# Second block: q's root mean square as a per-row scale of the attention's mask operation, norm weights applied at the eviction, rotary partners of q and k fetched by DMA

## The reference, cut to what matters

```python
def rmsnorm(x, g):
    xf = x.astype(jnp.float32)
    xf = xf * lax.rsqrt(jnp.mean(xf * xf, axis=-1, keepdims=True) + EPS)
    return (xf * g.astype(jnp.float32)).astype(x.dtype)

def rope(t, cos, sin):
    tf = t.astype(jnp.float32)
    t1, t2 = jnp.split(tf, 2, axis=-1)
    out = jnp.concatenate([t1 * cos - t2 * sin, t2 * cos + t1 * sin], axis=-1)
    return out.astype(t.dtype)

def diff_attention(q, k, v, lam):
    ...
        s = jnp.einsum('bqhcd,bkhcd->bhcqk', qblk, k).astype(jnp.float32) * scale
        s = jnp.where(mask, s, neg)
        p = jax.nn.softmax(s, axis=-1)
        a = p[:, :, 0] - lam * p[:, :, 1]
...
        xn = rmsnorm(h, norm1_gain[i])
        proj = xn @ w_in[i]
        q, k, v, u, gates = jnp.split(proj, splits, axis=-1)
```

## Time and profile before

| | |
|---|---|
| median of 3 runs (lowest, highest) | 2210.58 us (2198.4, 2211.85) |
| the profiled execution: its time, its span | 2207.66 us, 2205.9 us |
| TensorE busy, mean granted clock | 97% of the span, 0.986 |
| DVE, ACT, POOL busy | 49%, 40%, 42% |
| DMA | 194.99 MB, mean 88 GB/s |
| q and k phase, p = 0 to 31 | 1305.4 to 1463.8 us from the span's start |
| v, gated unit, projection, p = 32 to 59 | 1463.8 to 1572 us |
| attention and output | from 1572.5 us |

### The profile page before, as it was taken

One profiled execution on the slowest core, in us unless ns is written; L12 is line 12 of the kernel. 1 busy time (PEld: TensorE's weight loads), 2 busy tenths in 40 slices (PEclk: granted clock), 3 DMA queues, 4 the chain that ended last, 5 costly groups with the idle time before them and its releaser, 6 DMA issues.

```text
span 2205.9 us, 28059 instructions
## 1 busy us (share of the span) xinstructions
PE 2146.6 (97%) x10228; PEld 1689.7 (77%) x10228; DVE 1070.1 (49%) x1726; ACT 893.1 (40%) x1248; POOL 923.1 (42%) x306
## 2 busy tenths in 40 slices
PE   7999999999999998999999999999999899999999
PEld 6875788888888775888888887666666687888887
DVE  7854242222247635332222267857677723644645
ACT  5345462223243445543222343255466525332332
POOL 4523344444455322545654556323221245344442
PEclk9999999999999999999999999999999999999999
DMA  4422122322224311232232231111211222323232
GB/s 166 156 77 76 52 80 83 108 94 95 84 85 151 111 55 56 62 111 95 83 108 95 81 142 58 58 58 62 69 47 58 93 98 69 105 95 95 95 95 76
DMA packets 114679, 194.99 MB, mean 88 GB/s; under 512 B 4752, under 2 KB 50064, under 8 KB 114320
## 3 DMA queue, kind: packets, MB, share of 16 engines
q1 hardware_dynamic: 112992, 189.12, 26.0%
q10 hardware_dynamic: 1584, 4.53, 0.6%
HBM read 189.44 MB, written 8.12 MB: 90 GB/s over the span
## 4 chain that ended last, share of the span: by engine, by line
PE 75%; issue 17%; DVE 3%; POOL 3%; ACT 1%; DMA 0%; ACTq 0%; DVEq 0%; POOLq 0%; SPq 0%
PE bank L709 62%; PE bank L811 4%; POOL w_lo L516 3%; PE bank L820 2%; PE bank L1020 1%; PE bank L787 1%; PE bank L883 1%; PE bank L763 1%; PE bank L843 1%; PE bank L871 1%; PE bank L772 1%; PE bank L1034 0%; DVE act_lo L2041 0%; PE bank L913 0%; PE bank L1041 0%
## 5 line engine op out<-in xcount | busy, mean ns | idle before, releaser
L516 POOL TENSOR_TENSOR w_lo<-raw,w_hi 128x2048 fp32r<-128x2048 f32 (+1 forms) x167 | 742.0, 4443 | 1178.0 <-ACT w_hi L1361 1177.8
L709 PE MATMUL bank<-act_hi,w_hi 128*128 128x512 f32 x1488 | 600.8, 404 | 10.6 <-DVE act_lo L2041 5.4
L709 PE MATMUL bank<-act_lo,w_hi 128*128 128x512 f32 x1488 | 583.6, 392 | 0.0
L709 PE MATMUL bank<-act_hi,w_lo 128*128 128x512 f32 x1488 | 583.5, 392 | 0.0
L1361 ACT ACTIVATE w_hi<-raw 128x2048 fp32r<-128x2048 f32 (+1 forms) x170 | 314.0, 1847 | 560.0 <-PE bank L709 541.2
L709 PEld LDWEIGHTS bank<-act_hi,w_hi 128*128 128x128 f32 x1488 | 282.3, 190 | 86.5 <-issue 14.6
L709 PEld LDWEIGHTS bank<-act_lo,w_hi 128*128 128x128 f32 x1488 | 282.2, 190 | 61.6 <-issue 5.3
L709 PEld LDWEIGHTS bank<-act_hi,w_lo 128*128 128x128 f32 x1488 | 281.7, 189 | 60.7
L709 PE MATMUL bank<-h_hi,w_hi 128*128 128x512 f32 x704 | 279.4, 397 | 0.3 <-DVE x L2462 0.3
L709 PE MATMUL bank<-h_hi,w_lo 128*128 128x512 f32 x704 | 277.9, 395 | 0.0
L709 PE MATMUL bank<-h_lo,w_hi 128*128 128x512 f32 x704 | 277.9, 395 | 0.0
(11 more groups left out here) (361 smaller groups left out, 2733.2 us busy)
## 6 DMA issues: line engine op xcount, KB each, us to landing
raw<-in_w_up SPq DMA_DIRECT2D x32, 1024.0 KB, 5.4
raw<-in_w_down SPq DMA_DIRECT2D x32, 1024.0 KB, 5.0
raw<-in_w_in SPq DMA_DIRECT2D x26, 1024.0 KB, 5.0
raw<-in_w_up SPq DMA_DIRECT2D x44, 512.0 KB, 4.4
raw<-in_w_in SPq DMA_DIRECT2D x28, 768.0 KB, 4.4
raw<-in_w_out SPq DMA_DIRECT2D x12, 1024.0 KB, 5.0
raw<-in_w_down SPq DMA_DIRECT2D x22, 512.0 KB, 4.2
raw<-in_w_attn_proj SPq DMA_DIRECT2D x4, 1024.0 KB, 5.0
```

Of the source, the lines that this page charges most:

```text
L516: pool.tensor_tensor(m.w_lo[slot][:, 0:n], m.raw[slot][:, 0:n], m.w_hi[slot][:, 0:n].bitcast(F32), ALU.subtract).then_inc(s["split_ready"], 1)
L709: mm = pe.matmul(o, ll if i == 2 else lh, rl if i == 1 else rh, start=first and n == 0, stop=last and n == len(steps) - 1)
```

## The change

For q, the 8 mean jobs become two batches of "columns" (p = 9 and 17): 16 small matmuls each, with a 128x128 piece of a block's squares as the weights and two columns of the 1/64 matrix as the moving operand, so that the mean of each query and component is a number on the query's partition. Three small operations on ACT and three on DVE make 0.125 / root of all 64 columns at once (`column_root`), and this tile replaces the constant 0.125 in the attention's mask operation. For k, the mean jobs stay (`k_mean`, p = 22 to 42) but the block is normed after its rotation. Norm gains are applied by ACT when it empties the bank, beside a squaring of the same bank. The 16 permutation products are gone: ACT issues four DMAs per block, each of which copies 32 partitions of the block to their partner's place in `partner` (two buffers), and the sign is in the sine table. All three operations of the rotation read SBUF.

```diff
+    def q_columns(n):
+        pe.wait_ge(s["q_squared"], c.up("q_squared", 4))
+        fill(7)
+        for j in range(4):
+            for t in range(NT):
+                mm = pe.matmul(bank[7][:, 0:8 * NT].rearrange("p (c j t) -> p c j t", c=2, t=NT)[:, :, j, t], m.q_square[j][:, t * P:(t + 1) * P],
+                               m.blk64.rearrange("p (c d) -> p c d", c=2)[:, :, 0], start=True, stop=True)
+        mm.then_inc(s["full7"], 1)
...
-    def q_partner(j):
-        pe.wait_ge(s["q_normed"], c.up("q_normed"))
-        one(7, m.rot, m.q_root[j % 2][:])
...
-Q_JOBS = [12, 14, 16, 18, 20, 22, *range(24, 32), *range(35, 44), *range(48, 57)]
+COLUMNS_AT, COLUMN_ROOT_AT = (9, 17), 18
+K_AT = (22, 24, 26, 28, 30, 36, 38, 42)
+PARTNER_AT = (6, 7, 10, 10, 14, 15, 18, 18, 21, 22, 24, 26, 29, 34, 36, 40)
+ROTATE_AT = (8, 8, 12, 12, 16, 16, 20, 20)
...
+    def block_out(b, j):
+        full(b)
+        if j >= KD + 4:
+            act.wait_ge(s["q_normed"], j - KD - 3)
+        elif j >= 4:
+            act.wait_ge(s["q_columns"], j // 4)
+        act.activation(m.q_square[j % 4][:], bank[b][:], ACT.Square).then_inc(s["q_squared"], 1)
+        gain = m.lam[:, 6:7] if j < KD else m.scol[:, SC["kg"]:SC["kg"] + 1]
+        act.activation(block_of(j), bank[b][:], ACT.Copy, scale=gain).then_inc(s[f"free{b}"], 1)
+        freed(b)
+    def fetch_partner(j):
+        if j >= 2:
+            act.wait_ge(s["q_ready"], j - 1)
+        half = HD // 2
+        for r in range(0, P, half):
+            of = r + half if r % HD == 0 else r - half
+            act.dma_start(m.partner[j % 2][r:r + half, :], block_of(j)[of:of + half, :]).then_inc(s[f"partner{j % 2}"], 16)
...
+    def rotate(j):
+        x, partner = (m.q2 if j < KD else m.k2)[:, j % KD, :], m.partner[j % 2][:]
+        wait(f"partner{j % 2}", 4 * 16)
+        dve.tensor_tensor(partner, partner, m.sin, ALU.mult).then_inc(s["dve_step"], 1)
+        c.up("dve_step")
+        link(dve.tensor_tensor(x, x, m.cos, ALU.mult))
+        link(dve.tensor_tensor(x, x, partner, ALU.add), "q_ready" if j < KD else "dve_step")
+    def k_norm(j):
+        root, x = m.q_root[j % 2][:], m.k2[:, j, :]
+        use(7)
+        refine(7, root, m.q_square[j % 4][:], eps=0.0)
+        dve.sem_inc(s["q_normed"], 1)
+        link(dve.scalar_tensor_tensor(x, x, -0.5, root, ALU.mult, ALU.mult), "q_ready")
...
-                dve.tensor_tensor_reduce(m.att[4 * comp + i % 4][:, 0:n], bank[4 + comp][:, 0:n], m.mask[:, T - n:T], 0.125, 3.0e38,
+                dve.tensor_tensor_reduce(m.att[4 * comp + i % 4][:, 0:n], bank[4 + comp][:, 0:n], m.mask[:, T - n:T],
+                                         m.q_scale[:, h // 4, 4 * comp + h % 4, i % NT:i % NT + 1], 3.0e38,
                                          ALU.add, ALU.min, m.nmax[:, at_:at_ + 1]).then_inc(s[f"free{4 + comp}"], 1)
...
+    rope2[np.arange(P) % HD < half, 1] *= f(-1.0)
```

More of the change, by code:

```diff
@@ L1067, in hook @@
                 sums_out(blk)
[L1068 to L1070 removed]
+        for n in jobs_at(p, COLUMNS_AT):
+            q_columns(n)
+        for j in jobs_at(p, K_AT):
+            k_mean(j)
     spread()
@@ L1664, in block_of, with column_root, jobs @@
         return (m.q2 if j < KD else m.k2)[:, j % KD, :]
-    def q_square(j):
-        if j >= 2:
[L1669 to L1678, removed]
+    def block_out(b, j):
[9 more added lines that the diff above has]
+    def fetch_partner(j):
+        if j >= 2:
+            act.wait_ge(s["q_ready"], j - 1)
[3 more added lines that the diff above has]
+            act.dma_start(m.partner[j % 2][r:r + half, :], block_of(j)[of:of + half, :]).then_inc(s[f"partner{j % 2}"], 16)
+    def column_root():
+        root, power = m.q_scale[:], m.q_power[:]
+        act.wait_ge(s["q_columns"], 2)
+        link(act.activation(root, m.q_mean[:], ACT.Ln))
+        link(act.activation(root, root, ACT.Exp, scale=-0.5))
+        act.activation(power, root, ACT.Square).then_inc(s["rough_root"], 1)
+    def jobs(p):
+        for j in jobs_at(p, PARTNER_AT):
+            fetch_partner(j)
+        for n in jobs_at(p, COLUMNS_AT):
+            use(7)
+        if p == COLUMN_ROOT_AT:
+            column_root()
+        for j in jobs_at(p, K_AT):
             if j >= 2:
[L1681 to L1684, removed]
+                act.wait_ge(s["q_ready"], KD + j - 1)
+            else:
+                act.wait_ge(s["q_columns"], 3)
+            inverse_root(7, m.q_root[j % 2][:], m.q_square[j % 4][:], eps=0.0)
     def short_response():
@@ L1716, in functions @@
             use(6)
-        for n in q_jobs_at(p):
-            job(n)
+        jobs(p)
     def v2_out(g, t):
@@ L2355, in job, with q_columns, column_root @@
-    def job(n):
-        kind, j = q_job(n)
-        (q_norm if kind == "mean" else q_rotate)(j)
+    def q_columns(n):
+        full(7)
+        eps = m.eps_col.rearrange("p (j t) -> p j t", j=1).to_broadcast([P, 8, NT])
+        mean = bank[7][:, 0:8 * NT].rearrange("p (j t) -> p j t", t=NT)
+        dve.scalar_tensor_tensor(m.q_mean[:, n], eps, 1.0 / P, mean, ALU.mult, ALU.add).then_inc(s["free7"], 1)
+        freed(7)
+        dve.sem_inc(s["q_columns"], 1)
+        c.up("q_columns")
+    def column_root():
+        root, power = m.q_scale[:], m.q_power[:]
+        wait("rough_root")
+        link(dve.tensor_tensor(power, power, m.q_mean[:], ALU.mult))
+        link(dve.scalar_tensor_tensor(root, power, 3.0, root, ALU.subtract, ALU.mult))
+        link(dve.tensor_scalar(root, root, -0.5 * 0.125, None, ALU.mult), "q_columns")
@@ L2360, in arithmetic, with jobs @@
+    def jobs(p):
+        for j in jobs_at(p, ROTATE_AT):
+            rotate(j)
+        for n in jobs_at(p, COLUMNS_AT):
+            q_columns(n)
+        if p == COLUMN_ROOT_AT + 2:
+            column_root()
+        for j in jobs_at(p, K_AT):
+            rotate(KD + j)
+            k_norm(j)
     for p in range(32):
```

44 lines of the change are left out of this document (13 added, 31 removed).

## The result

The changed kernel takes **2178.81 us** (median of 4 runs, 2174.78 to 2183.98) against 2211.22 (4 runs) for the kernel before: ratio 0.987, 95% interval 0.9848 to 0.9891. Two later sets of the same kernel gave 2176.53 (ratio 0.9874, 0.9847 to 0.9901) and 2179.65 (0.9871, 0.9843 to 0.9899). The forecast was 2177, the range 2164 to 2196.

A forecast was written before the change was run, and what follows sets the result against it. TensorE, busy for 97% of the span, was taken as the bound. Stream -17.8, stops -12.1, clock -5.0 and +3.3, DVE +1.0 sum to -30.6 us from 2207.66: 2177 us, range 2164 to 2196.

The forecast's parts named there:

- TensorE's stream: TensorE's q and k work: 16 partner and 8 q mean jobs removed, 32 columns products added, net -17.8 us.
- The stops: TensorE's four waits at permutation products queued behind DVE on bank 7 all go, -12.1 us.
- under 2 us of waits for DVE: Sign that the forecast is right: PE's waits for DVE before the attention total under 2 us.
- DVE and the states: DVE's extra 9.3 us before the fourth state mostly fits into idle time; one near miss, +1.0 us, bounds 0 and about 12.
- rival (c): DVE bounds p = 8 to 31, rotations reading SBUF twice stand still under POOL's weight split: 2190 us, chance 0.15.
- The clock: Slow stretches behind three of four stops go, -5.0 us; the two added batches bring one clock fall, +3.3 us.
- rival (a): Nothing is given back: neither batch lowers the clock, and the earlier trace's fall goes too: 2169.5 us, chance 0.15.
- Rival (b): Both batches of columns run at half clock with a slow stretch after each, 14.4 us for 3.3: 2188 us, chance 0.13.
- ACT and the DMAs: ACT's partner DMA issues cost 0 on the path; landing takes 2 to 5 us, hidden.
- rival (d): Slower: partner DMAs at p = 8 to 30 land late, at 10 us +14: 2222 us, chance 0.03; sign: idle DVE ended by DMA.
- The attention: The mask operation's per-row scale costs DVE 0 to 0.05 us each, 64 times; 0 on the path, at most +3 us.
- The first score: Sign that the forecast is right: the attention's first score comes near 1542 us in the profile.

The follow-up runs named there:

- e3: Changed kernel with the partners of q and k again from TensorE's permutation products through bank 7, not by DMA: 2204.53 us, ratio 0.9983 to the kernel before.
- e6: Changed kernel with q's eight partner fetches one hook later, the rotations where they were: 2176.37 us, ratio 0.9847 to the kernel before.
- e5: Changed kernel with the constant 0.125 again in the attention's mask operation in place of the row's scale: 2176.21 us, ratio 0.9843 to the kernel before.
- e1: Changed kernel with each batch of 16 columns products replaced by one product of 32 moving columns: 2172.54 us, ratio 0.9838 to the kernel before.
- e8: Changed kernel with squares and block matrix as float32r, two k jobs one hook later, another scratch tile for k's root: 2166.62 us, ratio 0.9805 to the kernel before.
- e2: Changed kernel with the 32 columns products four at a time between dense stretches, not in two batches: 2177.1 us, ratio 0.9858 to the kernel before.
- e7: Changed kernel with two of k's mean jobs one hook later (p = 31 and 39): 2176.89 us, ratio 0.9846 to the kernel before.
- e9: Changed kernel with both batches of columns two hooks later (p = 11 and 19): 2180.25 us, ratio 0.9867 to the kernel before.

## Why the prediction was right

Its total (-30.6) stands beside -27.3 in the first profile (267.16 - 239.86), -29.5 on the mean of three (237.6) and -32.4 between the medians. It started from an execution 3.6 us under the median of before, so the time, 2177, came out 1.8 us from the median though the difference is off by as much the other way. The terms:

- **TensorE's stream**, -17.8 predicted, -20.4 measured (243.0 to 222.6). The unit prices held alone: columns 0.23 us (0.24), partner 0.89 in e3 (0.85). Put back one at a time the parts give 14.3 + 2.6 = 16.9, so some 3 us of the difference appear only with both (2.8 where profiles of like clock loss are compared); what they are is open.
- **The stops**, -12.1 predicted. They went, but idle time fell by 9.7, 6.4 and 6.2 us only in the three profiles. The step that failed is "ACT's root and DVE's first refine fit into that": k's mean waits 2.4 to 5.1 us for bank 7, and at the stop shown above the root was ready 4 us before DVE came to the refine. The sum left out the job's rotation ahead of it, and the weight split that holds one of its operations for 4 to 5 us. The mark "under 2 us of waits for DVE" was missed (2.4, 5.7, 5.9).
- **DVE and the states**, +1.0: 0, 0.6 and 0.8 us of wait at `sums_out`. Right, and with the blocked rotation in place (5.05 us beside a split of 4.55). The bound of "about 12" beside it does not come out of its own numbers: 9.3 us more work less the 3.2 that the state came early leave 6.1; with the 15.3 of rival (c) added and the 7.05 of idle time taken off it is some 14. The mark of under 10 us of idle DVE was met in two profiles (8.6, 9.1) and missed in the first (12.0). Rival (c)'s mechanism ran, its price didn't: at q's rotations no delay reached TensorE (e6), at k's jobs the blocked operations brought stops of 1.1 and 1.3 us. The Trainium skill (SBUF — State Buffer, Who interferes with whom) says that whichever of the two starts first holds the shared port for its whole instruction. The trace agrees: the split began at 1336.44, the rotation at 1336.48, and it ended 0.5 us behind the split.
- **The clock**, -5.0 and +3.3, together -1.7. The first profile shows 10.2 to 13.7, so +3.4, the mean of three 8.5, so -1.7. By place both terms hold on the mean of three. Behind 120 us the kernel before lost 5.1, all of it behind stops, the changed one 0, 1.7 and 0: -4.5. Up to 120 us the kernel before lost 5.1, the changed one 13.7, 5.1 and 5.1: +2.9. But that +2.9 is the mean of 8.6, 0 and 0 from one and the same code, so it is luck that +3.3 came near it; the term should have had a spread of its own. Two details were off: the kernel before had a second fall without a stop, behind its first `sums_in` (1.7 us), and the fall of the earlier trace rows went in two of the three profiles, as rival (a) had it. Rival (b) named the right places in the first profile, though not the sum.
- **ACT and the DMAs**, 0: right on the path. An issue takes 0.61 us, not 0.44, a block's four 2.44; landing 1.9 to 5.6 us, where 2 to 5 was taken. DVE waits 17 us for it, so it was not hidden from DVE as I said, and the mark of rival (d), an idle DVE ended by a DMA, is there. Its price isn't: a hook's delay (e6) costs TensorE nothing.
- **The attention**, 0: the mask operation takes 0.06 us more, and e5 shows no difference in time.
- **The first score** near 1542: 1547.4, 1539.9 and 1540.3.

So the total came out by sizes that offset each other: the stream's gain was underrated by 2.6 us, that of the idle time (-12.1 + 1.0) overrated by 1.4 to 4.9.

## What to carry to other kernels

Where TensorE is busy for 97% of the span, count its stream: products taken out or made shorter lowered the time (e1, e8), products put back raised it (e3), while edits that only moved waits (e2, e6, e7, e9) gave nothing that can be measured. Split a stretch into stream, idle time and clock lost before comparing two profiles: a single profile's clock can hide or feign 5 us, so look at which falls stand behind stops before calling them chance. A job that uses a shared bank is priced with the whole queue on it, the operations ahead of the one that frees it included: half of the change was worth 4 us alone and 9 to 13 beside the other half.

## What the runs showed of the hardware

- Within the stretch the clock loss came in steps: 1.7 us, from 3.4 us at 0.50, or several of these in a row, in all 13 profiles, and for one code it differed by 8.6 us.
- The granted clock fell to 0.50 with TensorE busy all the while, during or right behind `sums_in` (4.9 us) and the batches (3.5 us); behind the first `sums_in` in 12 of 13 profiles, behind the later ones in some, and in e1, without batches, at the fourth (5.1 us).
- It also fell within 2 us behind all five stops of 2.5 us or more that stand past the small matmuls (5.07, 2.51 and 2.51 before; 2.76 and 2.60 in e3), and behind two of some 35 shorter ones.
- A DVE operation with two SBUF inputs took 4.10 to 5.12 us in place of 0.69 beside a weight split on POOL of 4.55 to 4.98 (first profile, 1336, 1452 and 1478).
- A batch of two-column float32 products with 128x128 weights takes 0.22 us each at full clock (3.49 for 16), as float32r 0.11 (1.70 for 16).
- A DMA issued from ACT for a 32-partition piece held its queue for 0.61 us, where the loads of the earlier trace rows took 0.44.
